# Decode softmax with each row's own maximum, row blocks combined in the closing weights, and the S5 work of VectorE in parts

## The reference, cut to what matters

```python
def diff_attend(q, k, v, q_pos, k_pos, lam, subln_g, lambda_init):
    s = jnp.einsum('bqhcd,bkhcd->bhcqk', q, k).astype(jnp.float32)
    s = jnp.where(mask, s, NEG_INF)
    p = jax.nn.softmax(s, axis=-1)
    a = p[:, :, 0] - lam * p[:, :, 1]
    o = jnp.einsum('bhqk,bkhe->bqhe', a, v.astype(jnp.float32))
    o = o * lax.rsqrt(jnp.mean(o * o, axis=-1, keepdims=True) + EPS)
    ...
def s5_mix(u, h0_re, h0_im, a_re, a_im, log_dt, b_re, b_im, c_re, c_im, d_skip, w_glu, b_glu):
    lam_bar = jnp.exp(lam * dt)                       # 32 groups x 64 complex states
    b_bar = ((lam_bar - 1.0) / lam)[:, :, None] * b_c
    bu = jnp.einsum('gph,bsgh->bsgp', b_bar, uf.astype(jnp.complex64))
    a_cum, h = lax.associative_scan(combine, (a, bu), axis=1)
    y = jnp.real(jnp.einsum('ghp,bsgp->bsgh', c_c, h + a_cum * h0[:, None]))
    ...
```

## Time and profile before

| what | value |
|---|---|
| device time, three runs | 1457.52, 1459.25, 1462.02 us |
| profiled execution, its own time | 1464.86 us |
| span of the profiled execution | 1463.1 us |
| TensorE busy | 1279.2 us (87%), mean granted clock 0.94 |
| VectorE, ScalarE, GpSimd busy | 521.6, 248.5, 214.7 us |
| bytes moved | 458.31 MB, mean 313 GB/s |

### The profile page before, as it was taken

The page is one execution under the profiler, slowest core; times in us unless marked ns, Lnnn a source line. Parts: engine busy times, 40 slices in busy tenths (PEclk is TensorE's granted clock), DMA queues, the critical chain, the costliest instruction groups (busy, mean ns, idle before and its releaser), DMA issues.

```text
span 1463.1 us, 26568 instructions
## 1 busy us (share of the span) xinstructions
PE 1279.2 (87%) x9000; PEld 670.6 (46%) x9000; DVE 521.6 (36%) x1413; ACT 248.5 (17%) x476; POOL 214.7 (15%) x329
## 2 busy tenths in 40 slices
PE   7999999999869799998869999976899999999930
PEld 4545555554324346666544444433444444444410
DVE  2723543253365455553512111153122111121126
ACT  2101111121212233332212000000011111111111
POOL 2003140313100200000010000001122222222211
PEclk9999999999989999998999999976999999999975
DMA  9989998869968999999996998998899999999764
GB/s 364 329 310 293 321 294 283 272 198 298 298 227 304 352 338 363 365 315 323 331 387 228 330 336 293 322 349 321 277 324 371 360 354 363 361 363 366 256 211 179
DMA packets 185201, 458.31 MB, mean 313 GB/s; under 512 B 23953, under 2 KB 24337, under 8 KB 176530
## 3 DMA queue, kind: packets, MB, share of 16 engines
q1 hardware_dynamic: 163602, 390.21, 75.4%
q0 software_dynamic: 21504, 66.78, 13.8%
HBM read 421.92 MB, written 33.80 MB: 311 GB/s over the span
## 4 chain that ended last, share of the span: by engine, by line
PE 70%; DMA 12%; DVE 7%; SPq 5%; issue 3%; DVEq 2%; ACT 1%; POOL 0%; ACTq 0%; POOLq 0%
PE WA L1800 52%; PE SC L1800 7%; PE OD L1800 7%; DMA ring<-in_cacheK 6%; SPq L500 4%; DMA qpad<-h_scratch,idc 3%; DMA ring<-in_cacheV 2%; PE WA L2166 2%; DVE arena L1769 1%; PE WA L1919 1%; DVE arena L1782 1%; DVE st L1141 1%; PE WA L2126 1%; DMA arena<-y_scratch 1%; DVEq L1771 1%
## 5 line engine op out<-in xcount | busy, mean ns | idle before, releaser
L1800 PE MATMUL WA<-arena 128*128 128x512 f32 (+10 forms) x1440 | 353.4, 432 | 17.6 <-issue 7.2
L1800 PE MATMUL WA<-arena,xm 128*128 128x512 f32 (+3 forms) x816 | 313.6, 581 | 8.4 <-DMA arena<-in_w_out 6.5
L1800 PEld LDWEIGHTS WA<-arena 128*128 128x128 f32 (+2 forms) x1440 | 191.6, 195 | 155.0 <-issue 135.5
L1800 PEld LDWEIGHTS WA<-arena,xm 128*128 128x128 f32 (+1 forms) x816 | 124.4, 174 | 162.8 <-issue 154.7
L1800 PE MATMUL WA<-xm,arena 128*128 128x512 f32 x192 | 87.3, 603 | 1.7 <-ACT arena L958 1.3
L1800 PE MATMUL OD<-ring,sall 128*32 128x512 f32 x512 | 71.0, 670 | 15.0 <-DMA ring<-in_cacheV 15.0
L563 POOL TENSOR_TENSOR st<-st,consts 128x1 f32<-128x1 f32 (+2 forms) x18 | 13.8, 765 | 466.2 <-DVEq L1175 280.0
L1800 PE MATMUL OD<-ring,qpad 128*32 128x128 f32 x2048 | 67.9, 285 | 15.7 <-DMA ring<-in_cacheK 15.7
L1800 PEld LDWEIGHTS OD<-ring,qpad 128*32 128x32 f32 x2048 | 56.6, 114 | 35.9 <-DMA ring<-in_cacheK 18.4
L1800 PE MATMUL SC<-ring,qpad 128*32 128x128 f32 x2048 | 64.9, 278 | 9.1 <-DMA ring<-in_cacheK 9.0
L1712 DVE TENSOR_TENSOR xm<-WA,colw 128x960 f32<-128x960 f32 x16 | 18.5, 1158 | 147.2 <-PE WA L2166 147.2
(11 more groups left out here) (364 smaller groups left out, 1244.1 us busy)
## 6 DMA issues: line engine op xcount, KB each, us to landing
ring<-in_cacheK SPq DMA_DIRECT2D x512, 256.0 KB, 4.7
ring<-in_cacheV SPq DMA_DIRECT2D x512, 256.0 KB, 4.7
arena<-in_w_gu SPq DMA_DIRECT2D x16, 2048.0 KB, 9.8
arena<-in_w_dn SPq DMA_DIRECT2D x16, 1024.0 KB, 14.3
ring<-in_w_gu SPq DMA_DIRECT2D x8, 2048.0 KB, 10.3
xm<-in_w_gu SPq DMA_DIRECT2D x8, 2048.0 KB, 10.5
ring<-in_w_dn SPq DMA_DIRECT2D x8, 1024.0 KB, 14.8
xm<-in_w_dn SPq DMA_DIRECT2D x8, 1024.0 KB, 14.8
```

The source lines that it names most:

```text
L1800: return pe.matmul(out, lhsT, rhs, start=first, stop=last, **kw)
```

## The change

Three things change.

1. **Softmax of the decode passes.** The exponential now uses each partition's own maximum, so it no longer waits for the maximum over the four blocks. The own score (`m1`) is taken in the last turn of K, from a PSUM bank of its own, and most of the maximum is taken before the last scores are there; `m2` does the last 512 columns and the scaling. Exp runs in two halves. The first V unit waits for the first of four transposed pieces only. The maximum over blocks is made behind the first V units (`m3`, `m4`), and the ratio exp(own minus common maximum) is multiplied into the row sum and into the closing weights (`m4`, `m5`).
2. **S5 on VectorE.** `s5a` is cut in four parts, `bA` in two, `bH` in three, each a unit of its own, so that other units can stand between them.
3. **The plan** is made anew by the same rules from the new lists, so most units on all engines stand in other places.

The core of the diff:

```diff
-        dec += [(("m1", x), 0.8, [(dec[-1][0], 0.9)]), (("m2", x), 0.3, [(("m1", x), 3.3)]),
-                (("m3", x), 0.3, [(("m2", x), 1.0)]), (("pt", x), 2.3, [(("m3", x), 3.2)])]
+                    if (t, g, y) == (TURNS - 1, 0, 1):
+                        dec.append((("m1", x), 1.0, []))
+        dec += [(("m2", x), 0.0, [(dec[-1][0], 0.6)]), (("pt", x), 2.3, [(("m2", x), 3.0)])]
+        after = {0: (("m3", x), 0.2, []), 1: (("m4", x), 0.3, [(("m3", x), 1.3)]), 2: (("m5", x), 0.3, [(("m4", x), 1.8)])}
...
-    s5 = [(("s5a",), 0.0, [(("dprep",), 2.0)])]
+    s5 = [(("s5a", 0), 0.0, [(("dprep",), 2.0)])] + [(("s5a", p), 0.0, [(("s5a", p - 1), 10.0)]) for p in range(1, 4)]
...
-        s5 += [(("bH", n), 0.0, [(("bX", n, JQ - 1), 1.2)])]
+        s5 += [(("bH", n, 0), 0.0, [(("bX", n, JQ - 1), 1.2)]), (("bH", n, 1), 0.0, [(("bH", n, 0), 4.2)]),
+               (("bH", n, 2), 0.0, [(("bH", n, 1), 3.4)])]
...
@@ ScalarE
-            def m3(x):
+            def m2(x):
                 act.wait_ge(s_nb, x + 1)
-                act.activation(sall[:, :, :], sall[:, :, :], ACT.Exp, bias=mrow[:, 1:2], scale=HD ** -0.5,
-                               accum_out=mrow[:, 2:3])
...
+                for n in range(2):
+                    act.activation(sall[:, 2 * n:2 * n + 2, :], sall[:, 2 * n:2 * n + 2, :], ACT.Exp, bias=mrow[:, 1:2],
+                                   scale=HD ** -0.5, accum_out=mrow[:, 2 + 4 * n:3 + 4 * n])
...
+            def m4(x):
+                act.wait_ge(s_md, x + 1)
+                act.activation(mrow[:, 7:8], mrow[:, 5:6], ACT.Exp, scale=HD ** -0.5).then_inc(s_mf, 1)
...
@@ VectorE
+            def m2(x):
+
                 dve.wait_ge(s_evac, 2 * TURNS * (x + 1))
-                dve.reduce_max(mrow[:, 0:1], sall[:, :, :].rearrange("p t n -> p (t n)"), AX)
+                dve.reduce_max(mrow[:, 1:2], sall[:, TURNS - 1, :], AX)
                 dve.drain()
                 dve.tensor_tensor(mrow[:, 0:1], mrow[:, 0:1], mrow[:, 1:2], MAX)
+                dve.drain()
+                dve.tensor_scalar(mrow[:, 1:2], mrow[:, 0:1], -HD ** -0.5, None, MUL)
+                dve.drain().then_inc(s_nb, 1)
...
@@ TensorE
             def Vv(x, y, r, g, p):
...
-                    if y == 0:
-                        pe.wait_ge(s_ptw, x + 1)
...
+                if y + g + p == 0:
+                    pe.wait_ge(s_ptw, 5 * x + r + 1)
```

More of the change, by code:

```diff
@@ L94, in streams @@
                 for g in range(2):
-                    late = [(("pt", x), 1.2)] if t + g + y == 0 else [(("ov", b - 2), 1.2)] if t + g == 0 and y >= 2 else []
+                    late = [(("pt", x), 0.2)] if t + g + y == 0 else [(("ov", b - 2), 1.2)] if t + g == 0 and y >= 2 else []
                     dec.append((("V", x, y, t, g), 1.95, late))
+                    if y == 0 and 2 * t + g in after:
+                        dec.append(after[2 * t + g])
                     if y and t == 0 and g == 1:
@@ L259, in hymba_step @@
     SPOT, USES = banks(PLAN)
-    ready = {u: ends.get(u, ends.get(u[:-1], 0.0)) + (2.4 if u[0] == "S" else 0.0) for u in PLAN}
+    lag = {"S": 2.4, "m2": 1.5, "m4": 0.7}
+    ready = {u: ends.get(u, ends.get(u[:-1], 0.0)) + lag.get(u[0], 0.0) for u in PLAN}
     ACT_PLAN = sorted(PLAN, key=lambda u: ready[u])
@@ L424, in hymba_step @@
         s_mix = sem("s_mix")
[L425 to L426 removed]
+        s_score, s_evac, s_md, s_mf, s_mT, s_mrep, s_mb, s_nb, s_pexp = (sem(x) for x in (
+            "s_score", "s_evac", "s_md", "s_mf", "s_mT", "s_mrep", "s_mb", "s_nb", "s_pexp"))
         s_l, s_lP, s_ptw, s_pv, s_o4, s_aP, s_ad, s_ad2, s_dmix = (sem(x) for x in (
@@ L873, in pt, with s5a @@
                 act.drain().then_inc(s_ptw, 1)
-            def s5a():
-                act.wait_ge(s_ld5, 32)
-                act.activation(sm5[:, 0, :], par[:, 2, :], ACT.Exp).then_inc(s_act5, 1)
+            def s5a(p):
+                if p == 0:
+                    act.wait_ge(s_ld5, 32)
+                    act.activation(sm5[:, 0, :], par[:, 2, :], ACT.Exp).then_inc(s_act5, 1)
+                if p != 1:
+                    return
                 act.wait_ge(s_dve5, 1)
@@ L1354, in s5a, with bA @@
                     a, b = b, a
-            def bA(n):
-                if n:
-                    dve.wait_ge(*filled("Y", n - 1, 1))
-                else:
-                    dve.wait_ge(*filled("u", 3, 1))
-                    dve.wait_ge(s_ust[1], 32)
+                    if tab is T1 and k == 4:
+                        yield
+                yield
+            s5a_part = s5a_parts()
+            def s5a(p):
+                next(s5a_part)
+            def bA(n, p):
                 j = slice(JQ * n, JQ * n + JQ)
                 full = [128, JQ, CH, W5]
-                t = [tmp5[:, 512 * m:512 * m + 512].rearrange("p (j r h) -> p j r h", j=JQ, r=CH) for m in range(2)]
                 Lj = [Lp[:, m, :, j].rearrange("p k j -> p j k") for m in range(2)]
-                cmul([PB[:, m, :, :, :] for m in range(2)], [bc[:, 0, m, j, :].unsqueeze(2).to_broadcast(full) for m in range(2)],
-                     [x[:, :, 0:CH].unsqueeze(3).to_broadcast(full) for x in Lj], t)
-                dve.drain().then_inc(s_pA, 1)
+                if p == 0:
+                    if n:
+                        dve.wait_ge(*filled("Y", n - 1, 1))
+                    else:
+                        dve.wait_ge(*filled("u", 3, 1))
+                        dve.wait_ge(s_ust[1], 32)
+                    t = [tmp5[:, 512 * m:512 * m + 512].rearrange("p (j r h) -> p j r h", j=JQ, r=CH) for m in range(2)]
+                    cmul([PB[:, m, :, :, :] for m in range(2)],
+                         [bc[:, 0, m, j, :].unsqueeze(2).to_broadcast(full) for m in range(2)],
+                         [x[:, :, 0:CH].unsqueeze(3).to_broadcast(full) for x in Lj], t)
+                    dve.drain().then_inc(s_pA, 1)
+                    return
                 for m in range(2):
```

134 lines of the change are left out of this document (79 added, 55 removed).

## The result

The changed kernel takes 1490.19 us, the median of six runs (1488.09 to 1496.54), against 1460.63 us of the kernel before, measured beside it (six runs, 1457.12 to 1466.50). The ratio is 1.0207, 95% interval 1.0177 to 1.0237: slower by 2.1%. The forecast was 1451 us, range 1437 to 1466, with 0.17 for slower. It was wrong in direction and the time lies outside the range. The profiled execution takes 1491.18 us, its span is 1489.2. Ratios leave out executions more than 1.5% above the fastest of their kernel and are taken against the kernel before of the same session (medians 1460.63 to 1463.47), so they are not exactly the quotients of the medians printed here.

The account below looks back on a forecast made before the run. Stage A was taken as bound by TensorE and the DMA engines in turns, stage B by TensorE. Stage A gains about 15 us (13.0 and 2), the closing chain takes about half back: -8, median 1459.25 to 1451, range 1437 to 1466.

Parts of the forecast that it names:

- Where the kernel is bound: Stage B: TensorE; stage A: TensorE full from 770 to 950 us, DMA engines at 0.97 from 560 to 770.
- The softmax: Decode passes, stage A: pages move sooner after the last K unit; 2 us gain, bounds loss of 5 to gain of 8.
- waits that they covered may show: Stage A: projections that covered the softmax now stand behind V units, so waits may show; loss bounded at 5 us.
- The cut of the VectorE unit: Prompt tile 2, stage A: the 11.13 us wait before a transpose goes, plus 1.85 of clock; together 13.0 us.
- rival E: Stage A: an equally long stall comes before another S5 or prompt unit; within 4 us of before; chance 0.11.
- No wait on VectorE above 4 us stands nearby: Sign in prompt tile 2: the 11 us wait before a transpose is gone and none above 4 us is near.
- The last `out` unit: End of stage A: from about 950.7, by -13.0, -2 and +7.9 for V units now in front, to 943.6.
- From there to the first product: Closing of stage A: V stream ends at 974, routing out at 1003.0, first product at 1017.5 instead of 1025.54.
- Rival C: End of stage A: V stream's end sets the start, first product 41.7 us later; 1467 if it is 992; chance 0.17.
- The gather: Before stage B: first gather lands 11.7 us after issue; routing to first product 14.5 us, against 23.2 before.
- Rival B: Before stage B: slow gather, or longer `ids` and `lists`; routing plus 24.5 instead of 14.5; 1461, half 1456; chance 0.14.

Follow-up runs that it names:

- `old_order`: The changed kernel with all its new instructions, put in the order of the kernel before; 1467.85 us, ratio 1.0003.
- `softmax_only`: The changed kernel without the S5 hunks (`s5a`, `bA`, `bH` whole as before); 1489.58 us, ratio 1.0169.
- `s5_only`: The kernel before with only the S5 hunks of the diff, its decode softmax as before; 1478.90 us, ratio 1.0101.
- `ids_first`: The changed kernel with `ids` put in front of the last two V units again; 1495.44 us, ratio 1.0213.
- `after_pace72`: The changed kernel with the planner's PACE, the least distance between page units, at 7.2 instead of 7.1 us; 1475.99 us, ratio 1.0105.
- `late_v11`: The changed kernel with the first V unit of both passes planned 11 us after `pt` instead of 0.2; 1481.29 us, ratio 1.0128.
- `before_pace72`: The kernel before with the planner's PACE, the least distance between page units, at 7.2 instead of 7.1 us; 1470.09 us, ratio 1.0054.
- `dve_split`: The kernel before with only the last S5 group's `bH` spread in three parts on VectorE, TensorE's order untouched; 1456.68 us, ratio 0.9957.

## Why the prediction was wrong, step by step

**Where the kernel is bound.** Right for stage B and for 770 to 950. The reading "TensorE full, or pages full" missed that the two meet: the kernel before is even between the last `out` unit and the last V unit at the end of stage A.

**The softmax.** Right in itself, by TensorE's rows of the last K unit and the first V unit, which answer to the earlier trace rows:

```profile
288.08 1.95 PE L1855 MATMUL OD<-ring,qpad 128*32 128x128 f32 x64
...
302.54 1.92 PE L1855 MATMUL SC<-ring,sall 128*32 128x512 f32 x16
```

The V unit starts 12.5 us behind the K unit's end (forecast 12 to 16), and the DMA share between them is 0.95 (forecast over 0.6). What failed is what it was taken to be worth at the last `out` unit: "I take 2 us of gain, with bounds from a loss of 5 to a gain of 8". The prediction wrote that "waits that they covered may show" and bounded that at 5. The gap closed, and nothing of it arrived: `old_order` has the new softmax at 1.0003, and in the order that the new lists bring, the softmax hunks alone (`softmax_only`) cost 1.7%, about 25 us.

**The cut of the VectorE unit.** The term was 13.0 us. By itself it measured 6 us (1 to 11); in the order that the lists made of it, it became a wait of 9.8 us at `ot` (`s5_only`), which is the mechanism of the prediction's rival E (at +1.0%, not E's even time), or many waits of up to 5.2 us (the changed kernel). "No wait on VectorE above 4 us stands nearby" was wrong.

**The last `out` unit.** Forecast 943.6, measured 974.8. This one number carries the error: 31.2 us. All of TensorE's time up to it, the kernel before and then the changed kernel:

```profile
0.00:950.80 950.80, 859.51 (x7586) 468.17 (x7590) 382.22 (x1074) 181.38 (x356) 121.93 (x217) 0.96 0.90 311
0.00:974.80 974.80, 876.66 (x7644) 476.37 (x7648) 384.73 (x1089) 182.94 (x362) 122.39 (x217) 0.95 0.90 311
```

The forecast had idle time fall by 13 us (the wait and the softmax) and busy time rise by 6 (7.9 for the V units moved in front, less 1.85 of clock). Measured, idle time rose from 91.3 to 98.1 and busy time by 17.2. The V units in front are there (58 more matmuls, 7.9 us as forecast); by difference 9.3 us are left for products that took longer, with a mean granted clock of 0.95 for 0.96. In the second executions of both it is 6.4 us more idle and 21.4 more busy. So the step that failed is the pair of terms, -13.0 and -2: in the new order they came out as +16, some 7 us of it new waits and some 9 us slower products. The 17.3 us more of idle time in 425 to 600 are offset for the most part by 14.1 us less in 290 to 425, so that stretch is not where the loss is to be read.

**From there to the first product.** Forecast 73.9 us, measured 74.9. Within it, `rt1` stood behind `o4s` and `ids` behind the projection of the decode rows, as forecast. `ids` took 3.77 us instead of 6.5. Rival C counts 41.7 us from E, the end of the last pages' products, to the first product (its 20 us before run from 1005.6). In the changed kernel E is 1005.8 and the first product starts 43.9 us later, where C's sum gives 1047.5; the product with the token's own value alone took 1.91 us instead of 1.0. So C's chain is nearly right, but not for its reason: E was late because the prompt side was, and `rt0` ended at 1007.3, only 0.4 us before the last V unit let `o4s` go. With `ids` in front (`ids_first`) the first product came at 1053.0. The router of tile 7 is late in both, and the first product starts 75 and 77 us behind the last `out` unit.

**The gather.** Rival B did not happen: from the routing (1033.3) to the first product it is 16.5 us, where the forecast had 14.5 and B 24.5. GpSimd's rows for the first two gathers of the changed kernel, and the landing times of weights and gathers in 1025 to 1060 (median us from issue to landing):

```profile
1033.62 1.47 POOL L690 DMA_INDIRECT qpad<-h_scratch,idc  x1 [4.34 <-DVEq L1762]
1035.40 1.00 POOL L690 DMA_INDIRECT ring<-h_scratch,idc  x1 [0.31 <-issue]
```

```profile
arena<-in_w_gu SPq DMA_DIRECT2D x2, 2048.0 KB, 21.9
ring<-h_scratch,idc POOLq DMA_INDIRECT x1, 18.5
```

TensorE could use the first gather at 1046.54, 12.9 us after its issue, with all four sets of weights issued between 1033.3 and 1037.5; the second took 18.5. By the rule of the Trainium skill, "DMA: Bandwidth & Descriptors", section on queues, rings and completion order, as weighed in the prediction, each DMA engine takes turns between the queues that have work, so more weights behind each other in SP's queue should not lengthen a gather in GpSimd's. The trace agrees for the first (12.8 us to landing, 11.7 before with two sets); for the second it does not decide, since that one also had the first ahead of it in its own queue.

**Chances.** The rivals priced the page stream's end, the gather and the closing chain, but none had the prompt heads lose. That order is a cost of its own was named ("the projections are now behind V units") and given 5 us at most. That was the place for a rival on the slower side. C had 0.17 and named as its condition that the 13 us are not won, but with waits for pages in their place; E was late through the prompt side. That its sum comes within 2.2 us is in part luck.

**Not settled.** What in the new order does it. The early V units may act through projections that are missing between the prompt heads' waits; the waits on VectorE in 425 to 600 (29.5 us for 15.0) fit that. The idle time of that stretch, near 29 us at three different ratios, and `after_pace72`, which has the same order up to the 303rd unit and is only 5 us late at the last `out` unit, do not. No run kept the order of all else and moved the V units of one pass alone. Nor is it shown why some 0.6% remain at `late_v11` beyond the 9 us in its profile. Of the clock it is known what it took (by difference about 9 of the 24 us at the last `out` unit, 13.5 of 28 in the second executions), but not which gaps brought it down.

## What to carry to other kernels

Where a planner writes the order of all engines, compare first the new instructions in the old order, then the new order; here the instructions were worth 0.0% and the order 2.1%. Then measure a few neighbouring plans before believing one: one constant of the planner was worth 0.5% in the kernel before and 1.0% in the changed one. The planner here counts TensorE's costs and fixed delays and sees no queue on VectorE, so a wait that is taken from one unit can come back at the next (11.1 us at `T` became 9.8 us at `ot`). And when two chains end even, as the last `out` unit and the last page do here, a gain on one is worth nothing until the other moves too: `before_pace72` has its last `out` unit 9 us earlier and its first product 6 us later.

## What was not expected of the hardware

- A stretch of products with short waits between them can be granted less than full clock: in the changed kernel, where 22% of 425 to 600 is idle in waits of up to 5.2 us, it was 0.86, a mean between its levels of 1.2 and 2.4 GHz, against 0.96 with 12% idle in the kernel before. The Trainium skill, "TensorE: Matmul & The Clock Gate", Part 1 on the clock gate, says that activity releases the lower clock and idling brings it back; the changed kernel agrees. The amount of idle time alone does not set it: with 28.6 and 28.2 us idle in the same stretch, `late_v11` has 0.93 and `s5_only` 0.88, and `dve_split`, with less idle time than the kernel before, has 0.94.
- `ids`, 32 passes of 52 columns, took 3.77 us in both executions of the changed kernel and 7.07 us in every other run. The rows show the two clock levels, 0.50 in the kernel before and 1.00 in the changed one, where `ids` stands right behind 5.89 us of products:

```profile
993.46:1000.53 7.07, 7.07 (x36) 6.97 (x40) 2.46 (x10) 0.00 (x0) 0.00 (x0) 0.50 0.62 230
1025.25:1029.00 3.75, 3.74 (x36) 3.61 (x32) 2.08 (x6) 1.15 (x2) 0.28 (x1) 1.00 0.02 4
```

- The kernel before takes 1450.39 to 1473.75 us over 25 executions, while its two profiles agree within 0.1 us at the last `out` unit and the last V unit. Those of the changed kernel differ by 4 us there.
